# Chunk loop of a gated delta-rule mixer: the carried state comes off the values before the inverse is applied

## The reference, cut to what matters

```
m   = eye + bc * kk * dec * (1 - eye)          # lower triangular, one per chunk and head
u_t = triangular_solve(m, bc * vc)
w   = triangular_solve(m, (bc * exp(gam)) * kc)
def step(s, inp):
    u = u_c - w_c @ s
    o = q_c @ s + qk_c @ u
    s = ge * s + k_c.T @ u
```

## Time and profile before

| | us |
|---|---|
| median of 3 runs | 1646.29 (1642.82 to 1647.12) |
| span of the profiled execution, first to last instruction | 1641.5 |
| TensorE busy in it | 1487.8 (91%) |
| VectorE busy | 538.9 (33%) |
| ScalarE busy | 435.9 (27%) |
| GpSimd busy | 290.5 (18%) |

### The profile page before, as it was taken

The page is one execution under the profiler, slowest core; times in us unless marked ns, Lnnn a source line. Parts: engine busy times, 40 slices in busy tenths (PEclk is TensorE's granted clock), DMA queues, the critical chain, the costliest instruction groups (busy, mean ns, idle before and its releaser), DMA issues. The chain is left out here.

```text
span 1641.5 us, 34661 instructions
## 1 busy us (share of the span) xinstructions
PE 1487.8 (91%) x14240; PEld 979.1 (60%) x14240; DVE 538.9 (33%) x1270; ACT 435.9 (27%) x1227; POOL 290.5 (18%) x250
## 2 busy tenths in 40 slices
PE   8999999989998999999999857999999999999950
PEld 4666666657566677777777433566666655555530
DVE  2445544413325544455444360111111111111106
ACT  2211111131123344434443100222222222222224
POOL 0000000002124333343333001111111111111115
PEclk9999999989998999999999977999999999999985
DMA  7332233242316122221221187999999999999975
GB/s 257 87 94 70 67 81 81 55 147 82 108 63 247 33 78 103 88 99 46 78 84 40 64 350 275 350 384 375 380 377 371 384 368 384 385 378 382 381 265 217
DMA packets 120115, 334.71 MB, mean 204 GB/s; under 512 B 42808, under 2 KB 72424, under 8 KB 92648
## 3 DMA queue, kind: packets, MB, share of 16 engines
q1 hardware_dynamic: 111160, 306.88, 50.4%
q0 software_dynamic: 7728, 22.29, 5.8%
q10 hardware_dynamic: 1152, 4.52, 0.7%
HBM read 290.37 MB, written 48.14 MB: 206 GB/s over the span
## 5 line engine op out<-in xcount | busy, mean ns | idle before, releaser
L2191 PE MATMUL bank<-sb_arena 128*32 128x256 f32 x6336 | 357.3, 386 | 12.9 <-DMA sb_arena<-w 11.8
L398 PE MATMUL bank<-sb_arena 128*128 128x368 f32 x1056 | 330.6, 476 | 6.7 <-DMA sb_arena<-xT 6.7
L2191 PEld LDWEIGHTS bank<-sb_arena 128*32 128x32 f32 x6336 | 205.1, 112 | 153.9 <-DMA sb_arena<-w 13.8
L398 PEld LDWEIGHTS bank<-sb_arena 128*128 128x128 f32 x1056 | 201.7, 191 | 133.5 <-DMA sb_arena<-w_conv 6.7
L2214 PE MATMUL bank<-sb_arena 128*32 128x256 f32 x3168 | 177.1, 379 | 2.0 <-DMA sb_arena<-w 1.0
L2214 PEld LDWEIGHTS bank<-sb_arena 128*32 128x32 f32 x3168 | 102.7, 110 | 70.7 <-issue 2.5
L985 PE MATMUL bank<-sb_arena 128*128 128x512 f32 (+1 forms) x288 | 131.2, 595 | 6.3 <-DVE sb_rlog L1596 5.0
L2157 POOL DMA_INDIRECT d_acc<-sb_arena,sb_oidx x32 | 46.2, 1444 | 472.1 <-ACT sb_arena L2280 472.1
L2330 DVE SCALAR_TENSOR_TENSOR sb_arena<-sb_arena,bank 128x128 f32<-128x128 f32 x99 | 28.6, 288 | 297.3 <-ACT sb_arena L2266 297.3
L2266 ACT ACTIVATE sb_arena<-bank 128x128 f32<-128x128 f32 x99 | 27.5, 278 | 353.6 <-PE bank L2191 353.6
L782 PE MATMUL bank<-sb_arena 128*128 128x384 f32 (+1 forms) x288 | 96.5, 488 | 7.7 <-PEq L151 7.7
(11 more groups left out here) (346 smaller groups left out, 1750.0 us busy)
## 6 DMA issues: line engine op xcount, KB each, us to landing
sb_arena<-w SPq DMA_DIRECT2D x204, 1024.0 KB, 30.5
sb_arena<-w_conv SPq DMA_DIRECT2D x28, 512.0 KB, 4.7
sb_arena<-d_conv SPq DMA_DIRECT2D x7, 1792.0 KB, 7.3
d_conv<-sb_arena SPq DMA_DIRECT2D x22, 512.0 KB, 3.3
sb_arena<-d_gam SPq DMA_DIRECT2D x8, 768.0 KB, 4.1
d_x<-sb_arena SPq DMA_DIRECT2D x9, 512.0 KB, 2.6
sb_arena<-xT ACTq DMA_DIRECT2D x8, 552.0 KB, 9.6
sb_arena<-w_out SPq DMA_DIRECT2D x8, 512.0 KB, 7.0
```

Source lines behind the costliest of these rows:

```text
L398: last = e.matmul(bank[3 * r + s][:, 0:TN], wring[n % NV][:, k, :], xT[:, k, TN * s:TN * s + TN], start=(k == 0), stop=(k == KT - 1))
L2191: mm = e.matmul(bank[r][j * CG:(j + 1) * CG, 0:2 * P], xgT[:, k, g * CG:(g + 1) * CG], w13[s][quarter_of(j, r)][:, k, :], start=(k == 0), ...
```

## The change

In the steps that finish a chunk, TensorE multiplies keys by the state (`carried`), right after `prep_a`. VectorE multiplies the result by the negative decay of each row and adds it to the values in place (`right_side`), between `scales` and `lower`. Then the inverse multiplies that difference (`u_product`, four products where there were eight). The product of inverse and keys, its copy on ScalarE and the scaled keys on GpSimd remain for chunk 0 only, whose sample rows use them. The waits follow: `prep_b` waits for the last level of the chunk before, `prep_c` for the right side, GpSimd's `keys` for the keys-state product.

```diff
 def prep_b(i):
+    if i >= 2:
+        e.wait_ge(S["lv_xa"], lx(i - 1, levels_of(i - 1)))
+        e.wait_ge(S["lv_xb"], lx(i - 1, levels_of(i - 1)))
...
 def prep_c(i):
-    if i >= 1:
-        e.wait_ge(S["wt"], i)
+    if i == 1:
+        e.wait_ge(S["wt"], 1)
+    elif i >= 2:
+        e.wait_ge(S["rhs"], i - 1)
...
+def carried(p):
+    e.wait_ge(S["st"], p)
+    for h in range(GH):
+        last = e.matmul(G0[:, h * P:(h + 1) * P], cv[p % 2][:, 4 + h, :], St[:, h, :], start=True, stop=True)
+    last.then_inc(S["ks_ps"], 1)
 def u_product(p):
+    e.wait_ge(S["lv_xa"], lx(p, levels_of(p)))
+    e.wait_ge(S["lv_xb"], lx(p, levels_of(p)))
-    e.wait_ge(S["wt"], p + 1)
-    e.wait_ge(S["vt"], p + 1)
-    e.wait_ge(S["st"], p)
+    e.wait_ge(S["rhs"], p)
     for h in range(GH):
-        e.matmul(G1[:, h * P:(h + 1) * P], XT[:, h, :], vt[p % 2][:, h, :], start=True, stop=False)
-        last = e.matmul(G1[:, h * P:(h + 1) * P], qw[:, 1, h, :], St[:, h, :], start=False, stop=True)
+        last = e.matmul(G1[:, h * P:(h + 1) * P], XT[:, h, :], vt[p % 2][:, h, :], start=True, stop=True)
...
     if prep:
         prep_a(i)
     if post and not first:
-        wt_product(p)
+        carried(p)
...
# ScalarE's step
-    if post and not first:
-        wt_copy(p)
...
# VectorE
+def right_side(p):
+    e.wait_ge(S["ks_ps"], p)
+    e.wait_ge(S["vt"], p + 1)
+    for h in range(GH):
+        v = vt[p % 2][:, h, :]
+        last = e.scalar_tensor_tensor(v, G0[:, h * P:(h + 1) * P], coef[:, p, NEG + h:NEG + h + 1], v, ALU.mult, ALU.add)
+    last.then_inc(S["rhs"], 1)
...
     if prep:
         scales(i)
+    if post and not first:
+        right_side(p)
+    if prep:
         lower(i)
...
# GpSimd's keys(i)
-    if i:
-        e.wait_ge(S["wt_ps"], i)
-    e.tensor_tensor(kgn[0:n], ...)
+    if i == 0:
+        e.tensor_tensor(kgn[0:n], ...)
+    if i >= 2:
+        e.wait_ge(S["ks_ps"], i - 1)
     e.tensor_tensor(kd[i % 2][0:n], ...)
```

More of the change, by code:

```diff
@@ L595, in program @@
         sem("q2", "eg", "relu", "dm", "qd", "kT_ps", "kk_ps", "qk_ps", "vT_ps", "cb_ps", "xT_ps", "bT_ps", "a0_ps",
-            "ssk", "k_tok", "x_tok", "b_tok", "kse", "krc", "F", "kno", "kgn", "kd", "at", "a0", "x0", "xt0", "qkr", "qkm", "vt",
+            "ssk", "k_tok", "x_tok", "b_tok", "kse", "krc", "F", "kno", "kgn", "kd", "at", "a0", "xt0", "qkr", "qkm", "vt",
             "qse", "cbm", "cbd", "xdt", "xdte", "xd",
             "lv_bt", "lv_ya", "lv_yb", "lv_ysa", "lv_ysb", "lv_za", "lv_zb", "lv_xa", "lv_xb", "lv_ta", "lv_tb", "lv_xta", "lv_xtb",
-            "wt_ps", "wt", "u_ps", "u", "o_ps", "s_ps", "st", "oss", "qrc", "rq", "ots1", "ots2", "ote", "opw", "ogr", "og", "on",
+            "wt_ps", "wt", "ks_ps", "rhs", "u_ps", "u", "o_ps", "s_ps", "st", "oss", "qrc", "rq", "ots1", "ote", "opw", "og", "on",
             "yst_ps", "yin_ps", "h_ps", "ht", "sz_ps", "y1", "y2", "y4", "y5", "yss", "yse", "ypw", "yn",
@@ L602, in program @@
             "xa_ps", "xa", "xb_ps", "xb", "lg_ps", "rlog",
-            "m_zero", "m_seq", "m_c", "m_w", "m_q", "z_st", "p_out", "s_out", "z_mm", "z_sg", "z_ev", "l_zb0", "l_za0", "l_zc1", "l_wo",
-            "w_ps", "r_ps", "ss_m", "ss_ps", "ss_dec", "ss_new", "sm_ps")
+            "m_zero", "m_seq", "m_c", "m_w", "m_q", "z_st", "p_out", "z_mm", "z_sg", "z_ev", "l_zb0", "l_za0", "l_zc1", "l_wo",
+            "w_ps", "r_ps", "ss_m", "ss_ps", "ss_dec", "ss_new")
         sem("z_s0", "z_s1", "z_w0", "z_w1")
@@ L840, in prep_d, with sample_wt, u_product @@
                     last.then_inc(S["a0_ps"], 1)
-                def wt_product(p):
-                    n = n_of(p)
+                def sample_wt():
+                    e.wait_ge(S["lv_xa"], lx(0, levels_of(0)))
+                    e.wait_ge(S["lv_xb"], lx(0, levels_of(0)))
+                    e.wait_ge(S["kgn"], 1)
+                    for h in range(GH):
+                        last = e.matmul(G0[:, h * P:h * P + T0], kgn[0:T0, h, :], XT[0:T0, h, 0:T0], start=True, stop=True)
+                    last.then_inc(S["wt_ps"], 1)
+                def carried(p):
[3 more added lines that the diff above has]
+                    last.then_inc(S["ks_ps"], 1)
+                def u_product(p):
                     e.wait_ge(S["lv_xa"], lx(p, levels_of(p)))
                     e.wait_ge(S["lv_xb"], lx(p, levels_of(p)))
-                    e.wait_ge(S["kgn"], p + 1)
+                    e.wait_ge(S["rhs"], p)
                     for h in range(GH):
-                        last = e.matmul(G0[:, h * P:h * P + n], kgn[0:n, h, :], XT[0:n, h, 0:n], start=True, stop=True)
-                    last.then_inc(S["wt_ps"], 1)
-                def u_product(p):
-                    e.wait_ge(S["wt"], p + 1)
-                    e.wait_ge(S["vt"], p + 1)
-                    e.wait_ge(S["st"], p)
-                    for h in range(GH):
-                        e.matmul(G1[:, h * P:(h + 1) * P], XT[:, h, :], vt[p % 2][:, h, :], start=True, stop=False)
-                        last = e.matmul(G1[:, h * P:(h + 1) * P], qw[:, 1, h, :], St[:, h, :], start=False, stop=True)
+                        last = e.matmul(G1[:, h * P:(h + 1) * P], XT[:, h, :], vt[p % 2][:, h, :], start=True, stop=True)
                     last.then_inc(S["u_ps"], 1)
@@ L1075, in _ @@
                 e.wait_ge(S["y5"], 1)
-                wt_product(0)
+                sample_wt()
                 gate_part(8)
@@ L1189, in keys, with sample_wt_copy @@
                     last.then_inc(S["ssk"], 1)
+                    if i == 1:
+                        e.wait_ge(S["kgn"], 1)
                     if i:
-                        e.wait_ge(S["kgn"], i)
                         e.wait_ge(S["kd"], i)
                     e.activation(k_tok[0:n].rearrange("p h d -> p (h d)"), YA[0:n, :], ACT.Copy).then_inc(S["k_tok"], 1)
[L1195 to L1198, removed]
+                def sample_wt_copy():
+                    e.wait_ge(S["wt_ps"], 1)
+                    e.activation(qw[:, 1, :, 0:T0], heads(G0)[:, :, 0:T0], ACT.Copy).then_inc(S["wt"], 1)
                 def w_columns(h):
@@ L1313, in _ @@
                 gate_sigmoid(10)
-                wt_copy(0)
+                sample_wt_copy()
                 w_columns(0)
```

2 lines of the change are left out of this document (1 added, 1 removed).

## The result

The changed kernel takes 1651.71 us in the median of 8 runs (1647.82 to 1655.08), the kernel before 1645.34 us (1639.57 to 1647.65, 8 runs): a ratio of 1.0044, with an interval of 1.0028 to 1.0059. It is 6.4 us slower. The prediction was 1644.7 us with a range to 1650, and 0.12 for slower. The profiled executions have spans of 1648.0 and 1641.5 us, so they show the difference whole.

What follows compares the result with a forecast made beforehand. VectorE's queue was taken to bound each chunk step up to level 2, TensorE afterwards. Terms -0.8 - 7 x 0.22 + 0.7 = -1.6 us took the span from 1641.5 to 1639.9, shifted to 1644.7 us; range 1638 to 1650.

Steps and rivals of the forecast that it cites:

- the clock: TensorE's granted clock in steps 2 to 8: net effect taken as 0, bounds 5.4 us less to 8.4 us more.
- the trailing step: Chunk 8 finished, nothing prepared: the uncovered right side makes u_scale and all behind it 0.7 us later; bounds 0.5 and 1.0.
- What bounds a step: In a chunk step VectorE's queue sets the time until level 2 (617.10 us), TensorE afterwards.
- The products: On TensorE, four u products instead of eight per step: worth 0.93 us, 6.5 us over seven steps.
- The added right side: Four scalar_tensor_tensor on VectorE take 1.13 us and delay `lower` by 0.93 us per step; bounds 0.9 to 1.2.
- The hold: GpSimd's operations block VectorE's two-SBUF-tensor ones: of 0.95 us won at begin_x per step, 0.22 are left at level 2.
- the 0.22: Microseconds by which level 2 starts earlier in each of steps 2 to 8; bounds 0 to 0.95.
- Rival (a): VectorE and GpSimd don't hold each other, all 0.95 us reach level 2: -6.8, 1639.5 us; chance 0.16.
- Step 1: First chunk step, finishes nothing: GpSimd's missing multiply shortens L1453, 0.77 us won; bounds 0 and 1.0.
- Rival (b): Longer TensorE wait before L921 brings the 52.6 us kind of step each time: net +7, 1653 us; chance 0.12.
- The diff touches little else: Outside the chunk loop (steps 1 to 8 and two trailing steps, 500 to 949 us) the change touches little.

## Why the prediction was wrong

Three steps failed: the clock, which I put at 0 and which cost 2.9 us in the loop; the place of TensorE's code, which the sum had no term for (2.85 us in the profile, 4.7 by the medians); and the trailing step, where I priced the delay alone (2.1 us instead of 0.7). Step by step:

- *What bounds a step: VectorE's queue up to level 2.* Right; taking 0.7 us off it behind `begin_x` took 0.7 off each step. At the full clock the last thing of it that TensorE waits for is the operation behind level 2's start (L1424, a wait of 1.35 us in the kernel with three idle products), and not that start.
- *The products, 0.93 us per step.* Right; `u_product` is one group of four, 1.14 us, and no wait comes with `carried`.
- *The added right side, 0.93 us.* Right: `lower` starts 3.72 us into the step instead of 2.79.
- *The hold, 0.73 of 0.95 given back.* Right, to 0.1 us in each row: scores_b 1.53 (some 1.5 predicted), wait at ssd_inner 0.79 (0.85), level 2 at 17.56 (17.6). The 50.25 and 50.03 us of the kernels with idle products confirm the 0.22. Rival (a) is out. That rule of the Trainium skill, page "SBUF — State Buffer", section "SBUF: two separate sides", holds in the rows of both kernels.
- *Step 1, -0.8.* Right, but the first profile hides it. In the repeat of the changed kernel begin_xt takes 0.73 us instead of 1.46 and scores_b 0.68, from begin_x to ssd_inner it is 6.39 us where it was 7.11, and the step is 0.8 us shorter. The five other traces in which GpSimd's order is the changed kernel's have scores_b at 0.68 too. In the first profile the number (-1.3) has another reason. There GpSimd's earlier multiply freed begin_xt (0.83 us) and held scores_b instead (1.52), so that from begin_x to ssd_inner it is 7.33 us. What was won lies ahead of it, in the clock: the first keys-by-keys group runs in 1.06 us, before in 1.91 and in the repeat in 1.92 (rows below, first the kernel before, then the changed one), and begin_x comes 1.6 us earlier into the step. That clock is this execution's luck and not the change's work.

```profile
501.12 1.91 PE L794 MATMUL bank<-sb_arena 128*128 128x128 f32 x8
...
507.34 0.75 DVE L1446 TENSOR_TENSOR sb_arena<-sb_ident,bank 128x256 f32<-128x256 f32 x2 [1.73 <-PE bank L839]
```

```profile
501.05 1.06 PE L794 MATMUL bank<-sb_arena 128*128 128x128 f32 x8
...
505.86 0.75 DVE L1453 TENSOR_TENSOR sb_arena<-sb_ident,bank 128x256 f32<-128x256 f32 x2 [0.37 <-PE bank L844]
...
508.50 1.52 DVE L1475 TENSOR_TENSOR sb_arena<-sb_arena 128x512 f32<-128x512 f32 x1
```

- *The trailing step, +0.7.* The delay was 0.79. The step failed in its last word, that all behind it is merely later: TensorE stands 2.40 us in front of `u_product`, and the lower clock behind that cost another 1.3. I had priced the delay and not the wait.
- *The clock, 0.* This step failed. Rival (b) had the mechanism: a wait of 0.79 instead of 0.20 in front of ssd_inner and 2.02 behind it bring the lower level every time, and in step 2 as well, which I had held to be safe because of its 1.00. It had the size wrong: steps of 51.2 and not 52.6. In the 52.6 us step of the kernel before the lower level came later, behind the L881 of level 2 (1.14 us for eight), and still held L938 (1.75 us for four); in the changed kernel it is there from L890 on (2.05) and gone by L947 (1.03). It costs 2.9 us more than before. With 1.4 saved in the same steps and 0.8 to 1.3 in step 1 the loop alone would have been within 1 us of the kernel before. That rival (b)'s 1653 us lies near the 1651.7 measured is luck: it held nothing but the clock in the loop.
- *"The diff touches little else."* This step failed by a term that was left out altogether, and by the medians it is the largest single one. I counted each instruction that goes as time and none as place. The code behind the expert loop came to lie where TensorE stalls; the medians with and without padding are 4.7 us apart.
- 1.0 us that the first experts lose before the weights' DMA sets the pace has no experiment of its own. The third expert's up products take 12.88 us where they took 11.46, at the lower clock; what decides how long it lasts there stays open.

## What to carry to other kernels

When a change takes work off an engine that keeps waiting for another, price the wait as well as the delay: each longer wait on TensorE is a chance of the lower clock for what follows. Where a loop with branches comes later in the program, compare versions at the same program length, or at least look for idle time called "issue" behind the loop; some cheap instructions inside a long wait move it. And before you give VectorE's queue a shorter path, look at which GpSimd operation it will now meet: here moving one multiply was worth 10.4 us, where the change by itself had cost 6.4.

## What the runs showed of the hardware that I had not expected

- A stall of 2.4 to 3.6 us (2.46, 2.44, 3.20, 3.55) behind a loop that ends, at a place set by the length of the program ahead: none, or one behind 6, 8 or 9 product instructions (0.88 us behind 53). Adding 128 instructions removed it from one kernel and gave it to the other.
- The same stop of TensorE costs more than its length: 180 product instructions of 128x256 behind it took 9.92 us in one execution and 11.60 in another.
- Idle products give the clock back where the waits are. With one before and two behind ssd_inner the wait at level 2 fell from 2.02 to 0.25 us and steps 3 to 7 all became 50.03 us; four behind it outlasted the wait by 1.3 us and gave the same 50.03.
- What an execution's clock does at one place shifts VectorE against GpSimd at the next: the changed kernel's scores_b in step 1 took 1.52 us in one execution and 0.68 in its repeat.
